# Packed experts' later weight pieces in halves, and the wide experts' last down products moved

## The reference, cut to what matters

```python
def swiglu(x, wg, wu, wd):
    return (jax.nn.silu(x @ wg) * (x @ wu)) @ wd

def moe(x, router, wg, wu, wd):
    logits = (x @ router).astype(jnp.float32)
    top_logit, top_idx = lax.top_k(logits, TOP_K)        # 2 of 8 experts per token
    top_w = jax.nn.softmax(top_logit, axis=-1)
    gates = jnp.sum(jax.nn.one_hot(top_idx, N_EXPERTS) * top_w[..., None], axis=-2)
    y = jnp.zeros_like(x)
    for e in range(N_EXPERTS):
        y = y + gates[..., e:e + 1] * swiglu(x, wg[e], wu[e], wd[e])
    return y
```

## Time and profile before

| what | value |
|---|---|
| median of three executions | 2861.83 us |
| the profiled execution, its own time | 2859.74 us |
| its span, first to last instruction | 2858.0 us |
| outside the span | 1.74 us |
| TensorE busy with matmuls | 2701.2 us (95%) |
| VectorE, ScalarE, GpSimd busy | 1423.8, 486.9, 165.0 us |
| mean granted TensorE clock | 0.967 of full speed |
| mixture of experts on TensorE | about 1208 to 1830 us of the span |

### The profile page before, as it was taken

One profiled execution on the slowest core, in us unless ns is written; L12 is line 12 of the kernel. 1 busy time (PEld: TensorE's weight loads), 2 busy tenths in 40 slices (PEclk: granted clock), 3 DMA queues, 4 the chain that ended last, 5 costly groups with the idle time before them and its releaser, 6 DMA issues.

```text
span 2858.0 us, 42167 instructions
## 1 busy us (share of the span) xinstructions
PE 2701.2 (95%) x18698; PEld 2331.7 (82%) x18698; DVE 1423.8 (50%) x1886; ACT 486.9 (17%) x779; POOL 165.0 (6%) x155
## 2 busy tenths in 40 slices
PE   8999899999999989999999989999799989997998
PEld 5878788999687878896969648795699988876998
DVE  5773223895577322451314100167558766675454
ACT  1271111100127111110000000023111022122110
POOL 0002210000000221000000000000000001010000
PEclk9999999999999999999999999999799989998999
DMA  7442214885444221247474668634159634441442
GB/s 262 138 154 68 74 60 154 319 325 186 157 137 154 68 73 59 86 155 272 148 266 140 242 243 299 231 114 167 59 210 356 253 120 148 148 148 60 163 163 89
DMA packets 211925, 476.42 MB, mean 167 GB/s; under 512 B 7584, under 2 KB 36896, under 8 KB 211488
## 3 DMA queue, kind: packets, MB, share of 16 engines
q1 hardware_dynamic: 211168, 472.26, 46.9%
q10 hardware_dynamic: 576, 1.46, 0.1%
HBM read 472.64 MB, written 1.05 MB: 166 GB/s over the span
## 4 chain that ended last, share of the span: by engine, by line
PE 78%; issue 11%; DVE 5%; DMA 3%; ACT 1%; POOL 1%; SPq 0%; POOLq 0%; DVEq 0%; ACTq 0%
PE ps L1741 17%; PE ps L471 15%; PE ps L539 12%; PE ps L531 8%; PE ps L1989 4%; PE ps L1942 3%; PE ps L2259 3%; PE ps L2357 2%; DMA ring<-in_exp_w_up 1%; PE ps L1178 1%; PE ps L2287 1%; PE ps L1189 1%; PE ps L1185 1%; PE ps L2425 1%; DMA ring<-in_exp_w_down 1%
## 5 line engine op out<-in xcount | busy, mean ns | idle before, releaser
L471 PE MATMUL ps<-uT,ring 128*128 128x256 f32 x1024 | 237.7, 387 | 12.1 <-DMA ring<-in_w_in 9.4
L471 PEld LDWEIGHTS ps<-uT,ring 128*128 128x128 f32 x1024 | 194.4, 194 | 38.6 <-issue 9.3
L1741 PE MATMUL ps<-uT,ring 128*128 128x128 f32 x1584 | 193.8, 283 | 5.3 <-ACT uT L904 2.5
L1741 PEld LDWEIGHTS ps<-uT,ring 128*128 128x128 f32 x1584 | 189.7, 199 | 7.8 <-issue 7.5
L471 PE MATMUL ps<-xn,ring 128*128 128x256 f32 x768 | 174.2, 385 | 9.5 <-issue 6.9
L1741 PE MATMUL ps<-xn,work 128*128 128x128 f32 x1584 | 179.8, 275 | 0.0
L1741 PEld LDWEIGHTS ps<-xn,work 128*128 128x128 f32 x1584 | 178.3, 192 | 0.0
L471 PEld LDWEIGHTS ps<-xn,ring 128*128 128x128 f32 x768 | 146.7, 194 | 30.8 <-issue 11.3
L539 PEld LDWEIGHTS ps<-uT,ring 128*128 128x128 f32 x1344 | 158.3, 197 | 7.1 <-issue 6.8
L539 PE MATMUL ps<-uT,ring 128*128 128x128 f32 x1344 | 160.2, 280 | 2.5 <-ACT uT L904 2.5
L1791 ACT ACTIVATE work<-ps 128x512 f32<-128x512 f32 (+1 forms) x108 | 60.4, 559 | 405.0 <-PE ps L1741 405.0
(11 more groups left out here) (474 smaller groups left out, 4568.8 us busy)
## 6 DMA issues: line engine op xcount, KB each, us to landing
ring<-in_w_in SPq DMA_DIRECT2D x72, 1024.0 KB, 5.1
work<-in_ada_w SPq DMA_DIRECT2D x48, 1024.0 KB, 10.7
ring<-in_exp_w_down SPq DMA_DIRECT2D x40, 1024.0 KB, 7.1
ring<-in_attn_w_in SPq DMA_DIRECT2D x36, 1024.0 KB, 5.1
ring<-in_exp_w_gate SPq DMA_DIRECT2D x32, 1024.0 KB, 6.6
ring<-in_exp_w_up SPq DMA_DIRECT2D x32, 1024.0 KB, 7.4
ring<-in_ffn_w_in SPq DMA_DIRECT2D x32, 1024.0 KB, 7.5
ring<-in_ffn_w_out SPq DMA_DIRECT2D x22, 1024.0 KB, 8.4
```

The costliest lines, as they stand in the source:

```text
L471: mm = pe.matmul(acc[:, m * T:(m + 1) * T], w[:, k, m * P:(m + 1) * P], src[:, half * 4 + k, :], start=(half == 0 and k == 0 and m % 2 == ...
L1741: mm = pe.matmul(acc[:, m * P:(m + 1) * P], weights[:, k, m * P:(m + 1) * P], x[:, k, :], start=(start and m == 0 and k == 0), stop=True, ...
```

## The change

`stage_units` puts ("down", e-1, 2) between ("up", e, 0) and ("up", e, 1) for the second and third wide expert; the last expert's down 2 stays where it was. The order of the transfers follows it, as both come from the same list. `pack_turn_pe` moves from behind both pieces of down 1 to between them.

The pieces of steps 2 and 3 of each pack, and of steps 2 to 4 of rows, are loaded in two transfers of half a piece; those of the last rows step are one block and stay one transfer, but wait like a first half. The first half (blocks k = 0 and 1 of a pack step, block 0 of a rows step) waits for a new semaphore `pk_half`, raised when TensorE is done with the first half of the step two before; the second half waits for `slab_used` as before and raises a semaphore of its own, `slab_late`, for which TensorE waits in the middle of the step.

```diff
             for e in range(N_WIDE):
-                units += [("up", e, 0), ("up", e, 1), ("down", e, 0), ("up", e, 2), ("pack", e, e), ("down", e, 1), ("down", e, 2)]
-            return units + [("rows", 0, 0)]
+                units.append(("up", e, 0))
+                if e:
+                    units.append(("down", e - 1, 2))
+                units += [("up", e, 1), ("down", e, 0), ("up", e, 2), ("pack", e, e), ("down", e, 1)]
+            return units + [("down", N_WIDE - 1, 2), ("rows", 0, 0)]
...
+        def halved_slabs():
+            packs = [unit_slab(("pack", e, e)) + 6 + j for e in range(N_WIDE) for j in range(6)]
+            return packs + [unit_slab(("rows", 0, 0)) + 6 + j for j in range(12)]
...
+        def late_wait(pe, m):
+            n0 = ffn_at["ffn1"][0]
+            pe.wait_ge(slab_late[m % R], 16 * sum(n0 + j <= m and (n0 + j) % R == m % R for j in halved_slabs()))
...
                 elif g < 2:
-                    down_pe(pe, name, e, g)
+                    down_pe(pe, name, e, g, (0,))
                     if g == 1:
                         pack_turn_pe(pe, e)
+                    down_pe(pe, name, e, g, (1,))
...   pack_up_pe
                 for k in range(4):
+                    if step >= 2 and k == 2:
+                        for j in range(len(PACKED)):
+                            late_wait(pe, m + 3 * step + j)
...
+                    if k == 1:
+                        mm.then_inc(tick(pk_half), 1)
                 mm.then_inc(tick(slab_used, 3), 3)
...   pack_rows_pe
                 for k in range(min(2, FE - t0)):
+                    if i >= 2 and k == 1:
+                        for j in range(len(PACKED)):
+                            late_wait(pe, m + 3 * i + j)
...
+                    if k == 0 and t0 + 1 < FE:
+                        mm.then_inc(tick(pk_half), 1)
...   moe_sp, for the three pieces of a step
+                    if j0 + first in halved_slabs():
+                        sp.wait_ge(pk_half, steps_done - 2)
+                        for j, (r, piece) in step:
+                            ffn_load(sp, expert[r], (n + j0 + j) % R, piece, gate, up, down, 0)
+                        for j, (r, piece) in step:
+                            sp.wait_ge(slab_used, n + j0 + j - R + 1)
+                            if piece[0] != "d" or piece[2] == 2:
+                                ffn_load(sp, expert[r], (n + j0 + j) % R, piece, gate, up, down, 1)
+                        continue
```

More of the change, by code:

```diff
@@ L202, in build @@
         pk_pick, pk_silu, pk_mul, pk_turn = sem("pk_pick"), sem("pk_silu"), sem("pk_mul"), sem("pk_turn")
+        pk_half, slab_late = sem("pk_half"), [sem(f"slab_late{i}") for i in range(R)]
         cond_out, mod_out, y_out = sem("cond_out"), sem("mod_out"), sem("y_out")
@@ L3421, in _, with ffn_load @@
             run(stages())
-        def ffn_load(sp, e, slot, piece, gate, up, down):
+        def ffn_load(sp, e, slot, piece, gate, up, down, half=None):
             what, a, b = piece
             if what == "d":
-                dst = ring[:, slot, 0:b * D].rearrange("p (k c) -> p k c", c=D)
-                src = down(e, a * P, b * P).rearrange("a (k p) c -> p (a k) c", p=P)
+                lo, hi = (0, b) if half is None else (half, half + 1)
+                dst = ring[:, slot, lo * D:hi * D].rearrange("p (k c) -> p k c", c=D)
+                src = down(e, (a + lo) * P, (hi - lo) * P).rearrange("a (k p) c -> p (a k) c", p=P)
             else:
                 w = GROUPS[a] * P
-                dst = ring[:, slot, 0:4 * w].rearrange("p (k c) -> p k c", c=w)
-                src = (gate if what == "g" else up)(e, b * 512, sum(GROUPS[:a]) * P, w)
+                lo, hi = (0, 4) if half is None else (2 * half, 2 * half + 2)
+                dst = ring[:, slot, lo * w:hi * w].rearrange("p (k c) -> p k c", c=w)
+                src = (gate if what == "g" else up)(e, b * 512, sum(GROUPS[:a]) * P, w)[:, lo * P:hi * P, :]
                 src = src.rearrange("a (k p) c -> p (a k) c", p=P)
-            sp.dma_start(dst, src).then_inc(slab_in[slot], 16)
+            sp.dma_start(dst, src).then_inc((slab_late if half else slab_in)[slot], 16)
         def moe_sp(sp, n, gate, up, down):
@@ L3438, in moe_sp @@
             expert = [sp.value_load(by_rank[0:1, r:r + 1], min_val=0, max_val=EXPERTS - 1) for r in range(EXPERTS)]
[L3439 to L3442, removed]
+            steps_done = 0
+            for unit in stage_units():
+                pieces = unit_slabs(*unit)
+                j0 = unit_slab(unit)
+                for first in range(0, len(pieces), 3 if unit[0] in ("pack", "rows") else 1):
+                    if unit[0] in ("pack", "rows"):
+                        step = list(enumerate(pieces))[first:first + 3]
+                        steps_done += 1
+                    else:
+                        step = [(first, pieces[first])]
+                    if j0 + first in halved_slabs():
[7 more added lines that the diff above has]
+                        continue
+                    for j, (r, piece) in step:
+                        sp.wait_ge(slab_used, n + j0 + j - R + 1)
+                        ffn_load(sp, expert[r], (n + j0 + j) % R, piece, gate, up, down)
+            j0 = len(stage_slabs())
+            for j, (r, piece) in enumerate((r, piece) for r in SOLO for piece in ffn_slabs()):
+                sp.wait_ge(slab_used, n + j0 + j - R + 1)
+                ffn_load(sp, expert[r], (n + j0 + j) % R, piece, gate, up, down)
         @block.sync
```

## The result

The changed kernel takes 2821.72 us (median of four runs, 2820.64 to 2822.55) against 2863.64 us for the kernel before in the same series; the ratio is 0.9855 (95% interval 0.9841 to 0.9869). Forecast were 2824 us and a range of 2817 to 2836.

What follows compares the result with a forecast made beforehand. TensorE was taken as the bound, its pack waits set by when slots come free. Savings of 20.3 + 10.7 + 7.0 = 38.0 us took the profiled 2859.74 to 2821.7, the median to 2824; range 2817 to 2836.

Steps and rivals of the forecast that it cites:

- Part 1: Packs loaded in halves: TensorE's weight waits and the slow clock after them go, 20.3 us saved over three packs.
- Part 2: Rows loaded in halves: two waits and slow matmuls go, 10.7 us saved; the 2.16 us wait before the solo product stays.
- The halves' cost: 27 more transfers on SyncE's queue: extra time per half taken as 0, at most 2.35 us; added semaphore waits zero.
- Part 3: Moved down 2: P6's 2.65 us waits in group 1 of experts 1 and 2 go, with slow clock, 7.0 us saved.
- Cover (a): Next expert's group 0 pieces and VectorE's sums still arrive before P6 despite the moved down 2, with 8.3 us of slack.
- Cover (b): Group 1's four pieces, needing 2.6 + 10.8 us, land behind 14.5 us of group 0 and 10.5 of down 2.
- Part 4: The turn moved inside down 1: VectorE's products and ScalarE's copies stay covered, so zero effect.
- A: Rival: late halves still make TensorE wait in the halved steps, slow clock following some; price 10 us, 2834; chance 0.11.
- B: Rival: half transfers cost extra in the queue of the halved steps, slower from 0.7 us each; chance 0.05.
- C: Rival: the new order stalls P6 of group 0, so the move brings nothing or costs; 2831 to 2836; chance 0.05.
- D: Rival: the halves in packs and rows do nothing and only the moved down 2 gains; 2855 us; chance 0.03.

Runs made afterwards that it cites:

- experiment 7: Changed kernel with the turn put back behind both pieces of down 1; 2822.10 us, ratio 0.9857.
- experiment 9: The changed kernel run again as it is, beside a version with rows' full step last; 2820.73 us, ratio 0.9853.
- experiment 5: Changed kernel with first halves still issued early, but TensorE waiting for both halves at the start of each halved step; 2835.65 us, ratio 0.9908.
- experiment 4: Changed kernel with every half issued only when the whole step two before has ended and TensorE waiting for both halves; 2854.53 us, ratio 0.9965.
- experiment 1: Kernel before with only the moved down 2 and the turn inside down 1, no half transfers; 2854.59 us, ratio 0.9966.
- experiment 2: Kernel before with half transfers in steps 2 and 3 of the packs only, old order, rows as before; 2839.70 us, ratio 0.9916.
- experiments 6: Changed kernel with first halves issued only when the whole step two before has ended, TensorE still waiting one half at a time; 2836.07 us, ratio 0.9908.

## Why the prediction was right

**What bounds.** The slots' release, not the rate, held the packs up. The transfers' hole of 0.13 became a share of 0.63 and then 1.04, and TensorE's waits went from 20.9 us in packs and rows to 0.9.

**Part 1.** 20.3 us forecast, 20.4 measured, 20.1 alone. The schedule behind it was less good than its sum. The second halves of step 3 were to have 2.0 us of slack, and in pack 1 TensorE waited 0.32 us for them, so they came 2.3 us later than I had them. In pack 2 step 3's first halves came at T+16.2 and its second at T+19.2, where I had 14.4 and 17.5. In experiments 7 and 9, with the same packs, pack 1 has no wait, so the landing also scatters by some tenths. The term that was mis-sized is the landing of queued halves, taken as bytes over 387 GB/s plus 2.6 us; experiment 5 has it 0.8 us later already at the first step. It cost only 0.9 us because the slacks were about as large as the error, which is part luck. The wait of 0.74 us ahead of down 1 in pack 2, which I had left standing though my own schedule had the piece landing at T+21.2 and needed at T+21.2, went, and 0.61 us of waits for the two halves of step 3 stood in its place.

**Part 2.** 10.7 us forecast, 10.43 measured, 9.9 alone. The block took 38.68 us where I had 38.4. The wait of 2.16 us ahead of the solo product stayed as forecast (2.10).

**The halves' cost.** Forecast 0 between 0 and 2.35 us each; experiment 4 says 0 within 0.1. The extra semaphore waits cost nothing that shows: the block of 256 matmuls, with six of them inside, took 27.67 us, under twice the 13.94 of the earlier trace rows.

**Part 3.** 7.0 us forecast, 7.36 in the changed kernel and 7.4 alone. P6 of group 1 came 7.7 us after S4 (1394.37 against 1384.43 + 2.28); forecast 7.9. Cover (a) held by 6.8 us (P6 at 1358.99, S4 done at 1352.15) where I had 8.3, since S1 began at T+37.3 and not T+35.9. Cover (b) held as well: group 1's matmuls have no wait in them.

**Part 4.** Zero, and zero by experiment 7.

**The rivals.** A named the right place: late halves do make TensorE wait, but for 0.93 us in all, with no slow clock behind them, and not for 10. B falls by experiment 4, C by experiment 1, D by experiment 2.

**The sum.** The profiled executions differ by 2858.0 - 2820.8 = 37.2 us: 38.2 in the stretch, 2.8 us given back ahead of it (the first pack began at 1305.88 and not 1303.10) and 1.8 us gained behind it. The medians differ by 41.9. The runs of the kernel before say where the rest is: in the last series they lie between 2856.97 us, at a mean granted clock of 0.967, and 2866.82 us, at 0.963; the profiled one, at 2859.74 and 0.967, is among the fastest. The changed kernel's five lie within 3.2 us at 0.970 or 0.971. So the gain in the median seems to hold a few us of slow clock that other executions of the kernel before have and the profiled one has not. That these stand behind the removed waits is likely but not shown, as the trace of the kernel before is of one execution. I had worked from the profiled execution and added the 2.1 us to the median unchanged. For the profiled execution the forecast was 2821.7, and it took 2822.55, the slowest of its four; for the median it was 2824, 2.3 us too high. That both lie so near is in part luck, as the executions of the kernel before alone spread over 8 us.

## What to carry to other kernels

Where a consumer works in steps on several ring slots and frees them together, look at the transfers' share during the step after a stall: if it falls toward zero while all slots are full, the release is the bound, and it is worth trying to free in halves. Here, with bytes over rate (8.1 us) near the step's compute time (7.0 us), that won back all but 0.9 us of the waits. Early issue and a half-wise wait are two leads of the same kind: each alone took about two thirds of the gain here, and only both closed the gap. A small unit with no late inputs, such as a down product whose hidden values are long done, belongs between two groups whose second waits for another engine's sums.

## What the runs showed of the hardware that I had not expected

Six transfers of 0.5 MB that stand in SyncE's queue together took no longer than three of 1 MB: 397.59 against 397.44 us over a stretch with 27 more transfers. The Trainium skill's "DMA: Bandwidth & Descriptors", section "Anatomy of one DMA", gives about 2.0 us of fixed time to each transfer, for GpSimd's path. In this queue that part overlaps; experiment 4 shows none of it added.

From the moment at which the windows had a step's bytes moved until TensorE went on lay 0.9 us in the kernel before and in experiment 4, and 1.4 us in experiment 5, where the next step's halves were already queued. Slack reckoned from bytes and rate alone should leave room for it.

The granted clock after a short wait on TensorE falls in some cases and not in others. In one execution of the kernel before, after the same wait of 2.65 us, one P6 block took 10.96 us and another 12.59. The first solo product took 14.53 us after waits of 1.42, 1.76 and 2.04 us (experiments 6, 7 and 2) and 16.16 us after 2.05, 2.10, 2.15, 2.16 and 2.41 us (experiment 1, the changed kernel, experiment 4, the kernel before, experiment 9). Yet in experiment 5 the 64 matmuls after a wait of 2.19 us ran at full clock (5.37 us). The second window after the wait in the changed kernel:

```profile
1674.00:1676.00 2.00, 2.00 (x11) 2.00 (x11) 0.00 (x0) 0.00 (x0) 0.00 (x0) 0.50 1.05 386
```

and that of experiment 7's kernel:

```profile
1672.00:1674.00 2.00, 2.00 (x21) 2.00 (x20) 0.00 (x0) 0.00 (x0) 0.00 (x0) 1.00 1.05 386
```

Eleven matmuls started in the one and 21 in the other. Removing a wait of about 2 us was therefore worth its own length here, and 1.6 us more in some executions.
